# Between the two products of an MLP: when the first block's forms are read back, who splits them, and when the last pair's forms are made and stored

## What is computed

```python
def sq_relu_mlp(h, w_up, w_down):          # h: (T, 1024)
    a = jax.nn.relu(h @ w_up)              # w_up: (1024, 4096)
    return (a * a) @ w_down                # w_down: (4096, 1024)

xp = xp + sq_relu_mlp(rmsnorm(xp, norm_mlp[layer]), w_up[layer], w_down[layer])
```

## Time and profile before

| | |
|---|---|
| median of three runs | 3144.43 us |
| profiled execution, its own time | 3139.07 us |
| span from first to last instruction | 3137.2 us |
| PE busy | 3010.8 us (96%) |
| DVE busy | 1655.0 us (53%) |
| ACT busy | 1276.8 us (41%) |
| POOL busy | 1721.3 us (55%) |
| mean granted TensorE clock | 0.975 |

### The profile page before, as it was taken

One profiled execution on the slowest core, in us unless ns is written; L12 is line 12 of the kernel. 1 busy time (PEld: TensorE's weight loads), 2 busy tenths in 40 slices (PEclk: granted clock), 3 DMA queues, 4 the chain that ended last, 5 costly groups with the idle time before them and its releaser, 6 DMA issues. The chain is left out here.

```text
span 3137.2 us, 55917 instructions
## 1 busy us (share of the span) xinstructions
PE 3010.8 (96%) x22733; PEld 2790.1 (89%) x22733; DVE 1655.0 (53%) x2232; ACT 1276.8 (41%) x2202; POOL 1721.3 (55%) x1423
## 2 busy tenths in 40 slices
PE   8999999999999889998999999999998999989998
PEld 7998667777778889998999989998897999989998
DVE  4222365556553564446666617724446644566665
ACT  4211435566652344334444442313434334344443
POOL 1212103455431377878999615731114777899994
PEclk9999999999999999999999999999998999999999
DMA  6222205657653134436344124667430444453442
GB/s 221 55 83 73 73 21 183 221 209 242 222 216 105 27 119 151 147 130 211 133 154 140 71 93 146 224 219 285 168 121 24 147 137 144 144 201 134 142 146 78
DMA packets 298030, 451.81 MB, mean 144 GB/s; under 512 B 18496, under 2 KB 195584, under 8 KB 297520
## 3 DMA queue, kind: packets, MB, share of 16 engines
q1 hardware_dynamic: 277056, 357.44, 33.9%
q0 software_dynamic: 20000, 88.64, 8.0%
q10 hardware_dynamic: 720, 2.16, 0.2%
HBM read 318.37 MB, written 129.81 MB: 143 GB/s over the span
## 5 line engine op out<-in xcount | busy, mean ns | idle before, releaser
L112 PE MATMUL mlp_X<-mlp_f_hi,mlp_w_hi 128*128 128x272 f32 x1984 | 574.1, 289 | 16.5 <-DVE mlp_f_lo L940 13.2
L113 PE MATMUL mlp_X<-mlp_f_lo,mlp_w_hi 128*128 128x272 f32 x1984 | 573.9, 289 | 0.0
L114 PE MATMUL mlp_X<-mlp_f_hi,mlp_w_lo 128*128 128x272 f32 x1984 | 572.9, 289 | 0.0
L778 POOL TENSOR_TENSOR mlp_w_lo<-mlp_raw,mlp_w_hi 128x256 fp32r<-128x256 f32 (+1 forms) x348 | 341.2, 987 | 130.1 <-ACT mlp_w_hi L668 130.1
L112 PEld LDWEIGHTS mlp_X<-mlp_f_hi,mlp_w_hi 128*128 128x128 f32 x1984 | 375.3, 189 | 19.1 <-issue 14.4
L113 PEld LDWEIGHTS mlp_X<-mlp_f_lo,mlp_w_hi 128*128 128x128 f32 x1984 | 375.6, 189 | 0.0
L114 PEld LDWEIGHTS mlp_X<-mlp_f_hi,mlp_w_lo 128*128 128x128 f32 x1984 | 375.1, 189 | 0.0
L778 POOL TENSOR_TENSOR mlp_w_lo<-mlp_sums,mlp_w_hi 128x256 fp32r<-128x256 f32 (+1 forms) x286 | 316.4, 1106 | 24.0 <-DVE mlp_w_lo L866 14.8
L112 PE MATMUL mlp_Z<-mlp_f_hi,mlp_w_hi 128*128 128x272 f32 x992 | 287.3, 290 | 8.0 <-ACT mlp_ev L710 4.4
L113 PE MATMUL mlp_Z<-mlp_f_lo,mlp_w_hi 128*128 128x272 f32 x992 | 287.6, 290 | 0.0
L114 PE MATMUL mlp_Z<-mlp_f_hi,mlp_w_lo 128*128 128x272 f32 x992 | 287.1, 289 | 0.0
(11 more groups left out here) (578 smaller groups left out, 7661.2 us busy)
## 6 DMA issues: line engine op xcount, KB each, us to landing
hidden<-mlp_ev SPq DMA_DIRECT2D x224, 272.0 KB, 2.3
mlp_f_lo_plain<-hidden SPq DMA_DIRECT2D x112, 544.0 KB, 5.3
mlp_raw<-in_w_down SPq DMA_DIRECT2D x64, 512.0 KB
mlp_raw<-in_w_up SPq DMA_DIRECT2D x48, 512.0 KB
projections<-odd_zout SPq DMA_DIRECT2D x24, 544.0 KB, 4.2
forms<-gla_f SPq DMA_DIRECT2D x20, 544.0 KB, 2.7
residual<-xT SPq DMA_DIRECT2D x2, 4352.0 KB, 14.9
projections<-even_zout SPq DMA_DIRECT2D x16, 544.0 KB
```

Of the source, the lines that this page charges most:

```text
L112: pe.matmul(out, w_hi, x_hi, start=first, stop=False, skip_group_check=onto)
L113: pe.matmul(out, w_hi, x_lo, start=False, stop=False, skip_group_check=onto)
L114: return pe.matmul(out, w_lo, x_hi, start=False, stop=last, skip_group_check=onto)
L778: pool.tensor_tensor(to, x, y, op).then_inc(done_by, 1)
```

## The change

The loads of block 0's forms stand ahead of the last pair's stores in SyncE's list, except the store of form 1, which stays first. The stores of forms 5, 6, 7, 2 and 4 of the last pair go behind the weights that unit 1 issues. All seven forms of block 0 are split by VectorE, both halves at the same step as ScalarE's rounding, with steps 108, 109, 110, 111, 112, 114 and 116. `hidden_forms` of the last pair moves from step 111 to step 122 (in unit 1, behind the add of its product 6), `last_form` from 112 to 129 (the same place in unit 2). TensorE's waits count accordingly.

```diff
         def a_at(b, n):
             if b == 0:
-                return STEPS_UP - N + n + 3
+                return STEPS_UP - N + n + 3 + max(0, n - 4)
...
             load_down(0)
             store(1, m)
-            for n in range(3):
+            load_form(0, 0)
+            load_form(0, 1)
+            load_down(1)
+            for n in range(2, 5):
                 load_form(0, n)
-            load_down(1)
             load_down(2)
+            load_form(0, 5)
             store(3, m)
-            for n in range(3, 5):
-                load_form(0, n)
-            for p in (5, 6, 7):
-                store(p, m)
-            load_form(0, 5)
-            store(2, m)
             load_form(0, 6)
-            store(4, m)
...
                 if v + 3 < UNITS:
                     load_down(v + 3)
+                if v == 1:
+                    for p in (5, 6, 7, 2, 4):
+                        store(p, m)
@@ GpSimd @@
-            for b in range(BLOCKS):
+            for b in range(1, BLOCKS):
                 for n in ON_POOL:
                     lows.setdefault(a_at(b, n) + 1, []).append((b, n))
@@ VectorE @@
-            for b in range(BLOCKS):
+            for n in range(N):
+                for k in range(2):
+                    lows.setdefault(a_at(0, n), []).append((0, n, k))
+            for b in range(1, BLOCKS):
                 for n in ON_DVE:
...
-                    if p == 3:
+                    if p == 3 and m < PAIRS - 1:
                         hidden_forms(m)
                     if p == 4:
                         c21(m)
-                        last_form(m)
+                        if m < PAIRS - 1:
+                            last_form(m)
                 else:
                     down_add(*DOWN[i - 1 - STEPS_UP])
+                if i == STEPS_UP + N + 3:
+                    hidden_forms(PAIRS - 1)
+                if i == STEPS_UP + 2 * N + 3:
+                    last_form(PAIRS - 1)
@@ TensorE @@
-                    if n in ON_DVE:
-                        pe.wait_ge(alo_dve, 2 * (len(ON_DVE) * b + ON_DVE.index(n) + 1))
+                    if b == 0:
+                        pe.wait_ge(alo_dve, 2 * (n + 1))
+                    elif n in ON_DVE:
+                        pe.wait_ge(alo_dve, 2 * (N + len(ON_DVE) * (b - 1) + ON_DVE.index(n) + 1))
                     else:
-                        pe.wait_ge(alo_pool, len(ON_POOL) * b + ON_POOL.index(n) + 1)
+                        pe.wait_ge(alo_pool, len(ON_POOL) * (b - 1) + ON_POOL.index(n) + 1)
```

## The result

The changed kernel takes 3148.24 us, the median of 12 runs (3141.77 to 3154.33), against 3142.53 us for the kernel before (12 runs, 3136.87 to 3150.59). The ratio is 1.0018, with a 95% interval of 1.0009 to 1.0026: 5.7 us slower by the medians, 2.8 to 8.2 by the interval.

What follows compares the result with a forecast made beforehand. PE, busy all through, bounds the kernel; only its waits can shrink. First MLP -1.6 + 6.0 = +4.4, second -0.3 + 6.0 = +5.7, together +10.1 on 3144.43: 3154 us; own range 3146 to 3160, 8 in 10 3132 to 3166.

Steps and rivals of the forecast that it cites:

- The first wait stays: Last pair's product 3: ScalarE still waits for form (0, 0), so PE's 2.11 us and the clock behind stay; 0 change.
- The transfers cost nothing: Block 0's loads land before their turn, and weights behind the late stores arrive before use; cost 0.
- The chain of splits up to the first down add: VectorE's splits of forms 0 to 4 precede product 1's add; unit 0's product 6 waits 7.3 us, starting at 1447.5.
- Product 4 behind form 6: Unit 0's product 4 waits 1.8 us for product 7's add, which stands behind form 6's split on VectorE.
- The three subtractions in unit 1: Ahead of product 5's add they take 5.2 us, delaying unit 1's product 3; 6.0 us per MLP with clock and `last_form`.
- nothing more comes of it: GpSimd losing its three block 0 splits, some 8 us per MLP, brings nothing beyond the 1.8 us PE wait.
- Cheap splits: Rival, chance 0.22: VectorE's split halves take 0.64 us each, net -5.3 and -4.0 per MLP, total 3135 us.
- the stall gone: Rival, chance 0.08: only the first wait and its clock remain, the moved forms hide; 24 us go, total 3120.
- The moved forms dear: Rival, chance 0.20: each of unit 1's three subtractions takes 2.90 us, 8.7 in place of 5.2; total 3161.5 us.

Runs made afterwards that it cites:

- The kernel with the earlier load: Changed kernel with the loads of forms (0,0) and (0,1) ahead of the last pair's store of form 1: 3140.88 us, ratio 0.9991.
- the loads alone: Kernel before with only the loads of forms (0,3) and (0,4) put ahead of the store of form 3: ratio 1.0000.
- the kernel with the spread subtractions: Changed kernel with the last pair's three subtractions one at a time, at steps 121, 123 and 124, not all at 122: 3137.95 us, ratio 0.9982.
- each engine its own order: Changed kernel with earlier loads, spread subtractions and reordered splits, then ScalarE's rounding and VectorE's split steps chosen apart: 3115.97 us, ratio 0.9937 to the kernel before.

## Why the prediction was right, and where its sizes were off

The forecast was 3154 us, 10.1 more than before; measured were 5.7 (2.8 to 8.2) more, and 3.9 by the two traces. The mechanism was right, and every wait that was forecast came where it was said to; the terms ahead of unit 1 (the splits of forms 3 and 4, the wait before product 4) and that for the three subtractions were too dear. The 3154 also stands on a median of three runs, 3144.43, which twelve runs put at 3142.53.

- *The first wait stays.* It did, 2.37 and 2.26 us for 2.11 and 2.28. The kernel with the earlier load shows that it could have been taken away.
- *The transfers cost nothing.* The kernel with the loads alone bears it out for forms 3 and 4; for the late stores there is only the trace, without a wait there.
- *The chain of splits up to the first down add.* Product 6 was to start 23.4 us after product 7 and started after 22.4 and 22.3, behind a wait of 6.0 us and not 7.3. I had 2.35 us for every form. Forms 3 and 4 took 1.90 and 1.88: of each, the first half took 0.7 us and only the second the 1.25 that halves take beside GpSimd. Form 3's first half began in a pause of GpSimd's (0.20 us long); why form 4's was not slowed the runs do not show. The 2.34 us of VectorE's wait for ScalarE, expected as 1441.3 - 1438.95 = 2.35, were there.
- *Product 4 behind form 6.* A wait of 1.8 us was forecast and 0.58 came: form 6 took 1.36 us, with GpSimd idle. With this and the last point the front gained 3.4 and 2.5 us, not 1.6 and 0.3. This is the larger error, 4 us of the 6.2 by which the sum was too high.
- *The three subtractions in unit 1.* Forecast 5.2 us, 3.95 of wait, 1.87 for the clock, 0.2 for the last form: 6.0. Measured: 4.83 from 1466.92 to 1471.75, product 3 late by 3.4, 1.6 for the clock (products 3 and 4 took 4.64 us for 3.02), nothing for the last form: 5.0 and 4.85. One of the three met GpSimd's long split, 3.00 us; it was the last, where in the row that the 5.2 came from it was the first.
- *Cheap splits* and *the stall gone* did not happen. *The moved forms dear* neither: of the three, one met a long split.
- What the prediction had not seen is how much the move of GpSimd's splits was worth. I wrote that "nothing more comes of it" but the 1.8 us. Left on GpSimd beside the rest of the change they cost 6.1 us of place more, because product 3's relu and form 4's split then stand behind them. That worth depends on what stands around: with the three subtractions in their old place, all the rest of the change takes 93.8 us of place, the same as the loads alone on the kernel before. So it is the moved subtractions that make the change slower than the kernel before.

What stays open: why the medians of the kernel with the spread subtractions lie 10.3 us under the changed kernel's where the place gives 5.6 (the intervals of the two ratios leave room for that); and how the other 4.2 us arise by which the profiled executions differ (3145.3 us of span against 3137.2, of which the place gives 3.9); 4.6 us of difference stand ahead of the first place already.

## What to carry to other kernels

Work moved to an engine that is half idle on average goes into that engine's written order, and what counts is which instruction that others wait for comes next in it. Here the new order up to unit 1 gained 3.4 and 2.5 us over the old one, and the three subtractions in front of one later add lost 5.0 and 4.85. Loading earlier, spreading the subtractions and giving each engine its own order took the ratio from 1.0018 to 0.9937. Before a wait is called a bound by the amount of work, look whether the engine named has idle time in the same stretch, and for whom.

## What the runs showed of the hardware

- A VectorE instruction with both inputs in SBUF stood still while a GpSimd instruction that had started just before it ran: 2.98 us beside one of 2.49, 1.83 when that one was halved, 0.73 alone.
- TensorE can pay for a wait twice. After waits of 6.00 and 3.24 us, two down products took 5.07 and 4.64 us for 3.02, in stretches that lie partly at 1.2 and partly at 2.4 GHz: the granted clock, behind the busy times of the five engines, is 0.57 and 0.64.

```profile
1451.00:1456.20 5.20, 5.09 (x25) 5.09 (x26) 3.76 (x5) 1.83 (x3) 3.99 (x6) 0.57 1.06 384
1472.50:1477.20 4.70, 4.69 (x25) 4.69 (x26) 2.30 (x3) 0.42 (x1) 2.02 (x3) 0.64 0.33 122
```

- The length of the wait alone does not tell. After 1.82 us (the loads alone, before the last pair's product 3) the clock was 0.63 over the 4.65 us that the product took for 3.01. After 1.86 us (each engine its own order, before product 7) it stayed at 1.00, and the product took 1.77 for 1.51. After 0.58 us product 4 took 1.62, with the clock at 1.00 too.
